# Sample attention of a hybrid decoder step: keys and values of a cache entry loaded together in 4 KB rows into two buffers, in place of separate 2 KB rows into four

## What is computed

```python
GROUPS = ((128, 1), (512, 4), (2048, 16))      # window, dilation; PAST_LEN = 1024

def sample_dilated(q, kv_new, buf, g, bias):
    w, d = GROUPS[g]
    n_keys = w // d + 1
    kv_ext = jnp.concatenate([zeros(w), buf, kv_new], axis=1)
    k_ext, v_ext = kv_ext[:, :, 0], kv_ext[:, :, 1]
    ...
    return dilated_attend(q, k_ext, v_ext, q_idx, min_valid, d, n_keys, bias)

def merge_groups(outs, lses):
    wts = jax.nn.softmax(jnp.stack(lses, axis=0), axis=0)
    return jnp.einsum('gbth,gbthd->bthd', wts.astype(outs[0].dtype), jnp.stack(outs, axis=0))
```

## Time and profile before

| What | Value |
| --- | --- |
| median of 3 runs | 2612.0 us (2605.59 to 2615.58) |
| profiled execution | 2601.04 us |
| its span, first to last instruction | 2599.2 us |
| mean granted TensorE clock | 0.981 of full speed |
| PE busy | 2451.6 us (94% of the span) |
| DVE, ACT, POOL busy | 1144.8, 773.9, 227.6 us |
| DMA packets, bytes | 365137, 305.89 MB, mean 118 GB/s |

### The profile page before, as it was taken

The page is one execution under the profiler, slowest core; times in us unless marked ns, Lnnn a source line. Parts: engine busy times, 40 slices in busy tenths (PEclk is TensorE's granted clock), DMA queues, the critical chain, the costliest instruction groups (busy, mean ns, idle before and its releaser), DMA issues.

```text
span 2599.2 us, 44116 instructions
## 1 busy us (share of the span) xinstructions
PE 2451.6 (94%) x18487; PEld 2314.0 (89%) x18487; DVE 1144.8 (44%) x1460; ACT 773.9 (30%) x899; POOL 227.6 (9%) x179
## 2 busy tenths in 40 slices
PE   6999999988999999999999999999887779999998
PEld 5999999965899999987789999999676559999998
DVE  5444433767654443323244443333565445444322
ACT  2333312211433332111133332211453323333211
POOL 3000012101210000110000000120000012000021
PEclk9999999999999999999999999999999889999999
DMA  4444532544144443213464444223416942222330
GB/s 112 145 145 145 161 89 66 156 121 122 53 146 153 145 150 95 86 57 109 127 207 145 144 144 134 78 75 117 111 37 205 269 115 80 81 81 83 95 88 36
DMA packets 365137, 305.89 MB, mean 118 GB/s; under 512 B 10871, under 2 KB 328319, under 8 KB 364155
## 3 DMA queue, kind: packets, MB, share of 16 engines
q1 hardware_dynamic: 359883, 237.46, 32.3%
q0 software_dynamic: 5184, 67.43, 7.6%
HBM read 285.51 MB, written 70.54 MB: 137 GB/s over the span
## 4 chain that ended last, share of the span: by engine, by line
PE 86%; DVE 5%; DMA 2%; issue 2%; SPq 1%; ACT 1%; POOL 0%; POOLq 0%; DVEq 0%; ACTq 0%
PE ps L1228 71%; PE ps L1462 2%; PE ps L1463 2%; PE ps L1464 2%; DMA tb<-kvs 2%; PE ps L1520 2%; PE ps L1343 1%; SPq L453 1%; PE ps L1498 1%; DVE hL L861 1%; DVE cT L989 1%; PE ps L1558 1%; PE ps L1510 1%; PE ps L1501 0%; DMA ta<-kvs 0%
## 5 line engine op out<-in xcount | busy, mean ns | idle before, releaser
L853 DVE TENSOR_TENSOR wL<-wst,wH 128x1024 fp32r<-128x1024 f32 (+1 forms) x304 | 423.7, 1394 | 902.3 <-ACT wH L625 901.0
L1228 PE MATMUL ps<-hH,wH 128*128 128x288 f32 x3264 | 701.9, 297 | 17.4 <-DVE hL L861 13.5
L1228 PE MATMUL ps<-hH,wL 128*128 128x288 f32 x3264 | 698.1, 296 | 0.0
L1228 PE MATMUL ps<-hL,wH 128*128 128x288 f32 x3264 | 697.8, 296 | 0.0
L625 ACT CAST wH<-wst 128x1024 fp32r<-128x1024 f32 (+1 forms) x304 | 339.4, 1117 | 1003.9 <-PE ps L1228 837.1
L1228 PEld LDWEIGHTS ps<-hH,wH 128*128 128x128 f32 x3264 | 526.2, 189 | 22.6 <-issue 10.9
L1228 PEld LDWEIGHTS ps<-hL,wH 128*128 128x128 f32 x3264 | 526.2, 189 | 0.0
L1228 PEld LDWEIGHTS ps<-hH,wL 128*128 128x128 f32 x3264 | 526.0, 189 | 0.0
L1228 PE MATMUL ps<-actL,wH 128*128 128x288 f32 x1408 | 300.2, 295 | 0.0
L1228 PE MATMUL ps<-actH,wH 128*128 128x288 f32 x1408 | 300.1, 295 | 0.0
L1228 PE MATMUL ps<-actH,wL 128*128 128x288 f32 x1408 | 300.1, 295 | 0.0
(11 more groups left out here) (206 smaller groups left out, 2116.5 us busy)
## 6 DMA issues: line engine op xcount, KB each, us to landing
wst<-in_ffn_w_in SPq DMA_DIRECT2D x176, 512.0 KB, 3.8
wst<-in_ffn_w_out SPq DMA_DIRECT2D x64, 704.0 KB, 4.5
out_kv_sample<-in_cache_kv_w POOLq DMA_DIRECT2D x8, 4064.0 KB, 14.4
out_kv_sample<-in_cache_kv_w POOLq DMA_DIRECT2D x8, 2016.0 KB, 8.3
wst<-in_conv_w_pw SPq DMA_DIRECT2D x24, 512.0 KB, 3.9
wst<-in_w_kv SPq DMA_DIRECT2D x24, 512.0 KB, 3.8
uV<-ucat SPq DMA_DIRECT2D x80, 105.5 KB, 2.2
kvs<-kvst POOLq DMA_DIRECT2D x6, 1024.0 KB, 5.6
```

Source lines behind the costliest of these rows:

```text
L853: nc.vector.tensor_tensor(wL[:, s % 2, 0:size], wst[:, s, 0:size], wH[:, s % 2, 0:size].bitcast(f32), ALU.subtract).then_inc(S["w_ready"], 1)
L1228: nx = nc.tensor.matmul(outs[t], a, b[:, t, :], start=start and first, stop=stop and b is xh and not first)
```

## The change

Keys and values of an entry go to one buffer, kvA or kvB, of shape 128 x 9 x 2 x 512: tile, key or value, 512 numbers. The DMAs take 4 KB rows (keys and values of a position), so each of the 6 cache DMAs moves twice the bytes, and the two DMAs for the new rows stay as they were. All 8 count on kc_in0 or kc_in1 (128 an entry), and vc_in0 and vc_in1 go. Since a buffer holds both, a load of entry b waits for the product of entry b-2 alone. kvA lies where the weight buffers wst, wH and wL are in other stages, kvB where kcB and vcB were. Entry 0 is loaded behind the wait that its values had. The multiplications and copies are the same.

```diff
-    kcB, vcB, kTs = place("kcB", [P, 9, AW]), place("vcB", [P, 9, AW]), place("kTs", [P, PAIRS, SC])
+    kvB, kTs = place("kvB", [P, 9, 2, AW]), place("kTs", [P, PAIRS, SC])
...
-        def cache_rows(b, kv):
+        def cache_rows(b):
-            dst, new, sem = ((kc[b % 2], kn[b % 2], f"kc_in{b % 2}"), (vc[b % 2], vn[b % 2][:], f"vc_in{b % 2}"))[kv]
-            sp.dma_start(dst[:, 0:4, :], c512[b, :, :, kv, :]).then_inc(S[sem], 16)
+            dst, sem = kvc[b % 2], S[f"kc_in{b % 2}"]
+            sp.dma_start(dst[:, 0:4].rearrange("p k v n -> p k (v n)"),
+                         c512[b].rearrange("p k v n -> p k (v n)")).then_inc(sem, 16)
             for k in range(4):
-                sp.dma_start(dst[:, 4 + k, :], c2048[b, k, :, 0:NT, kv, :]).then_inc(S[sem], 16)
-            sp.dma_start(dst[:, 8, :], c128[b, :, kv, :]).then_inc(S[sem], 16)
+                sp.dma_start(dst[:, 4 + k].rearrange("p v n -> p (v n)"),
+                             c2048[b, k, :, 0:NT].rearrange("m t v n -> m t (v n)")).then_inc(sem, 16)
+            sp.dma_start(dst[:, 8].rearrange("p v n -> p (v n)"), c128[b].rearrange("p v n -> p (v n)")
+                         ).then_inc(sem, 16)
             r0 = (SEQ + NT * b) * 3
-            sp.dma_start(new, kvs3[r0:r0 + 24, kv * AW:(kv + 1) * AW]).then_inc(S[sem], 16)
+            for kv, new in enumerate((kn[b % 2], vn[b % 2][:])):
+                sp.dma_start(new, kvs3[r0:r0 + 24, kv * AW:(kv + 1) * AW]).then_inc(sem, 16)
...
-                cache_rows(0, 0)
                 sp.wait_ge(S["w_ready"], CB["wo"])
-                cache_rows(0, 1)
+                cache_rows(0)
...
-        cache_rows(1, 0)
-        cache_rows(1, 1)
+        cache_rows(1)
         for b in range(2, NB):
-            sp.wait_ge(S["ktr"], 12 * (b - 1))
-            cache_rows(b, 0)
             sp.wait_ge(S["pv2"], b - 1)
-            cache_rows(b, 1)
+            cache_rows(b)
...
-            pe.wait_ge(S[f"kc_in{o}"], (i + u // 2) * 112 + 112)
+            pe.wait_ge(S[f"kc_in{o}"], (i + u // 2) * 128 + 128)
...
-                pe.wait_ge(S[f"vc_in{u}"], i * 112 + 112)
...
-                        a = vc[u][:, k, cols] if k < 9 else vn[u][:, cols]
+                        a = kvc[u][:, k, 1, cols] if k < 9 else vn[u][:, cols]
```

More of the change, by code:

```diff
@@ L201, in trunk_program @@
     at[0] = w_at
-    vcA, vnA = place("vcA", [P, 9, AW]), place("vnA", [24, AW])
-    assert at[0] <= w_at + 4 * SLOT * 4
-    vc, vn = (vcA, vcB), (vnA, vnB)
+    kvA, vnA = place("kvA", [P, 9, 2, AW]), place("vnA", [24, AW])
+    assert at[0] <= w_at + 8 * SLOT * 4
+    kvc, vn = (kvA, kvB), (vnA, vnB)
     kn = [t[0:24].rearrange("p a b -> p (a b)")[:, 0:AW] for t in (ta, tb)]
@@ L214, in trunk_program @@
     at[0] = max(at[0], prompt_end)
-    kcA = place("kcA", [P, 9, AW])
     assert at[0] <= H0 + 2 * KD * TOK * 4
-    kc = (kcA, kcB)
     at[0] = H0
@@ L260, in trunk_program @@
         b_in0 b_in1 kt_tr kt_d kt_a qc_zero qc_a qc_d s_done s_evac sm_ready p_ready pt_done
-        pt_ready pv_done o_evac ot_done ot_ready kc_in0 kc_in1 vc_in0 vc_in1 ktr ktd kta ss_mm sm2
+        pt_ready pv_done o_evac ot_done ot_ready kc_in0 kc_in1 ktr ktd kta ss_mm sm2
         p2 os_ready ot2 ptr_d ptr_a ptr_mm pv2 o2 yg_ready yt y_ready dve_self act_self pool_self""".split()
@@ L1557, in transposes @@
                     for k in range(4):
-                        nx = nc.tensor.transpose(ps[:, bank, k * P:(k + 1) * P], kc[o][:, 4 * x + k, cols], ident[:])
+                        nx = nc.tensor.transpose(ps[:, bank, k * P:(k + 1) * P], kvc[o][:, 4 * x + k, 0, cols], ident[:])
                 else:
-                    nc.tensor.transpose(ps[:, bank, 0:P], kc[o][:, 8, cols], ident[:])
+                    nc.tensor.transpose(ps[:, bank, 0:P], kvc[o][:, 8, 0, cols], ident[:])
                     nx = nc.tensor.transpose(ps[:, bank, P:P + 24], kn[o][:, cols], ident[0:24, 0:24])
```

## The result

| | before | after |
| --- | --- | --- |
| median of 4 runs each | 2612.6 us | 2702.4 us |
| range | 2605.6 to 2615.6 | 2699.6 to 2709.5 |
| profiled execution (span) | 2601.0 (2599.2) | 2703.8 (2702.0) |

What follows compares the result with a forecast made beforehand. In sample attention the transfers, not PE, were taken as the limit. First wait +6.2 us, then six cycles of 16.5 + 12.4 = 28.9 us against 109.0 before: +70.6 us, so 2683 us; range 2655 to 2717.

Steps and rivals of the forecast that it cites:

- rival B: Sample attention loads: row width doesn't matter, rate stays at 282 GB/s, a load takes 19.6 us, +92.6 us, 2705; chance 0.20.
- Entry 0: Its load now waits on w_ready in full; over 130 us of prompt attention cover the shift: zero, uncovered some 20 us.
- the number of issues: SP issues 8 DMAs an entry in place of 14; worth nothing, as the data are behind the issues either way.
- the wait on the values that goes: The vc_in wait at the product goes; VectorE's copy of the probabilities released the product, so this frees nothing.
- The serial cycle L + C: Sample attention: load and compute in series, six cycles of 16.5 + 12.4 = 28.9 us, against 109.0 us for six before.
- C: Part of a sample attention cycle from the keys' first transpose to the end of the product: 12.4 us.
- L: From a load's issue to the keys' first transpose: 4.817 MB at 343 GB/s, 14.0, plus 2.5 fixed, 16.5 us.
- The first wait: Entry 1's load, with sbias ahead of it: transposes start at 1988.9 us against 1982.67, +6.2 us.
- the product of entry 0: It ends 12.0 us after the first wait, as before, so at 2000.9 us; the six cycles follow.
- the 378 of the earlier trace: GB/s in the best 2 us of before's sample attention; the fast bound, giving a load of 15.2 us.
- 3.1 us of cover: Sample attention: the keys are issued at the product's end and PE wants them 3.1 us later, under a load of over 14.
- both bounds named as a sign of error: Load bursts in sample attention above 400 or below 260 GB/s would show the prediction wrong.

Runs made afterwards that it cites:

- rows2k_late: Kernel before, with the keys of entry b issued only behind the wait for the product of b-2; four buffers and 2 KB rows stay: ratio 1.011 to before.
- rows2k_late_joint: As rows2k_late, and the key transposes of an entry also wait for its values, still 2 KB rows in four buffers: ratio 1.0355 to the kernel before.
- product_first: Changed kernel, with probability transposes and product of entry b-1 put ahead of the key transposes of b, matching copies reordered: ratio 1.0086 to the kernel before.
- chunked: Changed kernel, with a semaphore for each cache's part of the load and key transposes ordered by cache: ratio 1.032 to the kernel before.
- keys_three: Kernel before, with a third key buffer, keys issued one entry earlier and the sample loop written out: ratio 0.9958 to before, 11 us faster.
- before_contig: Kernel before, with the window 2048 cache DMAs reading positions 0 to 511 in a row (wrong positions, same bytes): ratio 0.9925 to before, 20 us faster.

## Why the prediction was right, and where it was off

The time was within the range, 19 us above the forecast of 2683. The mechanism was the one forecast; a term of the sum was too small. The measured 2702 lies above the 2674 to 2697 that the forecast's own chance of 0.56 stood for, and next to rival B's 2705, which had 0.20. By its own steps:

- Entry 0, the number of issues, and the wait on the values that goes were priced at nothing. The stretch behind the stage is unchanged (495.5 us), and the lead lost and the joint wait alone, in 2 KB rows, give the changed kernel's time (1.0355 and 1.036; stages of 218.5 and 222.4 us), so about 4 us of the stage are left for these three and the wide rows together, no more than two executions of before differ by (5 us).
- The serial cycle L + C is what the trace has: six cycles of 30.7 to 32.4 us, for 28.9. rows2k_late, rows2k_late_joint and product_first, which take the lead away and give the overlap back, show it as the cause.
- C was priced at 12.4 and came out at 12.5 on average over six (from 2037.69, 2068.54 and four more to the next load's issue).
- L was priced at 16.5 and is 19.05 on average (20.25 the longest, 18.57 the shortest). **This is the term that was too small, for its rate of 4 KB rows: 343 GB/s were supposed, and the loads moved at about 406 and then at 251.** Six times 2.55 are 15.3 us of the 18.7 by which the stage is longer than forecast. The first wait is 20.0 us for 18.3 (1.7 more), the product of entry 0 came 13.3 us behind it for 12.0, with more of it at the slower clock (1.2 more), C gives 0.5.
- Rival B, that the rows don't matter, was right about the rows: its L of 19.6 and its 2705 are nearer than my own numbers. I took the output weights' 343 GB/s as the nearest row, but that load reads another source, and its rate says nothing on this one; and the 378 of the earlier trace rows was no lucky stretch: in one-microsecond steps before's rate swings between up to 399 and some 230 to 280 GB/s, as the two caches take turns, and the 282 is the mean.
- Of the rules of the Trainium skill that the prediction weighed, the trace bears out the one against the change (DMA: Bandwidth & Descriptors, "Rules for kernel authors"): with 3.1 us of cover the stage grew by 89 us. The one for it (Perfetto Trace Analysis, "DMA Optimizations": larger transfers, such as 2 KB made 4 KB, can be much faster) does not hold for rows of 2 and 4 KB here: 410 against 406 GB/s in the one pattern, 260 against 251 in the other. The 408.7 GB/s that the Trainium skill lists (DMA: Bandwidth & Descriptors, "SWDGE vs HWDGE vs iDMA") is met, at 406 to 418, but only outside the 8-of-16 pattern.
- Of the profile's other signs these came: 9984 packets fewer, bursts at a DMA share of 1.0, a mean share of a half, a slower clock at the start of each entry's transposes. Those that hang on L were missed: cycles were over 30 us, and the six waits 15.4 to 17.2 us for some 13. The rate in the bursts broke both bounds named as a sign of error, above 400 in the one part and below 260 in the other; what it showed wrong was the single rate, not the series of load and work.

## What to carry to other kernels

Merging two loads merges their buffers' lifetimes and their waits: ask from which moment the joint buffer is free and who waits for the last byte, before asking what the wider row gains. Where a stage is bound by transfers, resolve the rate in time within one load: a mean over different source patterns is the rate of none. And when a wait sits ahead of independent work in an engine's order, moving that work first can give back most of what the lost buffers cost.

## What the runs showed of the hardware

- Loads of 8 rows of 4 KB (or 2 KB in each 4) out of every 16 moved at 230 to 260 GB/s with all DMA engines busy, the same bytes from both halves of each 64 KB at 400 to 420. The distance between the blocks (64 or 192 KB) made little difference (251 and 238 GB/s; stages of 222.4 and 221.7 us).
- Rows of 2 KB taken from every second 2 KB were as fast as full rows of 4 KB (up to 410 against 406 GB/s, and 259 to 261 against 251).
- After waits of 10.5 to 17.2 us PE ran its first 12 to 24 long transposes (128x128) at 1.2 GHz and the rest, with the product, at 2.4; where that work was itself broken by waits (chunked), the product 18 us behind the first of them still began at 1.2 GHz.
- In two of thirteen profiles (the first of before, and that of keys_three) PE issued 2003 and 2002 multiplications from 830 to 1090 us, in the others 1952 or 1953; in three others (before_contig, rows2k_late, rows2k_late_joint) it issued 2310 from 1400 to 1700 us, where the rest have 2252 or 2253. All at the same granted clock of 1.00. So five of thirteen executions ran one such part 2.6% faster. What sets this isn't seen in a trace. The ratios come from timed runs, not from these profiles.
